# A turn's sum of squares in the second input projection: two additions on GpSimd, one product with ones, made in the next turn

## What is computed

```python
proj = h @ w_in                       # split into q_lat, kv_lat, k_rope, x_lru, g_lru
xc = conv1d(x_lru, conv_w) + conv_b   # four taps along the tokens
r = sigmoid(xc @ w_a + b_a); i = sigmoid(xc @ w_x + b_x)     # per head, blocks of 128
log_a = -8 * r * softplus(-lam);  a = exp(log_a)
b = sqrt(max(1 - exp(2 * log_a), 0)) * (i * xc)
hh = scan(a, b)                       # h[t] = a[t] * h[t-1] + b[t]
lru = hh * gelu(g_lru)                # 512 wide
mixed = concat(rms_norm(attn, attn_out_norm), rms_norm(lru, lru_out_norm))
```

## Time and profile before

| | us |
|---|---|
| median of 3 runs | 4268.16 |
| lowest, highest | 4266.77, 4273.60 |
| span of the profiled execution | 4260.5 |
| the stage `second_projection` in it | about 2348 to 2884 |

### The profile page before, as it was taken

The page is one execution under the profiler, slowest core; times in us unless marked ns, Lnnn a source line. Parts: engine busy times, 40 slices in busy tenths (PEclk is TensorE's granted clock), DMA queues, the critical chain, the costliest instruction groups (busy, mean ns, idle before and its releaser), DMA issues. The chain is left out here.

```text
span 4260.5 us, 53668 instructions
## 1 busy us (share of the span) xinstructions
PE 3916.6 (92%) x17927; PEld 2473.8 (58%) x17945; DVE 1735.5 (41%) x3722; ACT 1457.9 (34%) x3219; POOL 594.5 (14%) x757
## 2 busy tenths in 40 slices
PE   6999999799889977999998999969999897899998
PEld 4677667455765535777776777745666454333333
DVE  1343344566555550101111577773333445333332
ACT  1122122455444411111110566653333222344443
POOL 0000000100530011111111000000000001333332
PEclk8999999899999968999999999989999998899999
DMA  6221221222434566665654222132231233698963
GB/s 231 82 79 68 94 88 48 90 81 87 149 128 165 177 233 233 203 193 189 205 172 137 63 65 65 60 89 69 60 99 39 94 128 144 216 301 274 290 202 74
DMA packets 228403, 581.86 MB, mean 137 GB/s; under 512 B 28394, under 2 KB 99306, under 8 KB 212382
## 3 DMA queue, kind: packets, MB, share of 16 engines
q1 hardware_dynamic: 176702, 395.74, 27.1%
q0 software_dynamic: 51552, 184.18, 14.5%
HBM read 437.60 MB, written 142.12 MB: 136 GB/s over the span
## 5 line engine op out<-in xcount | busy, mean ns | idle before, releaser
L2135 PE MATMUL out_psO<-out_w,out_mixT 128*128 128x512 f32 x1024 | 449.6, 597 | 3.3 <-ACT out_mixT L2107 1.8
L878 PE MATMUL inp_psU<-inp_w,inp_hT 128*128 128x512 f32 (+3 forms) x1376 | 420.8, 464 | 0.0
L3968 PE MATMUL moe_psU<-moe_wu,moe_xT 128*64 x768 | 345.7, 604 | 6.4 <-issue 5.6
L3970 PE MATMUL moe_psU<-moe_bu,moe_xT 128*64 128x512 f32 x768 | 345.7, 604 | 0.0
L878 PEld LDWEIGHTS inp_psU<-inp_w,inp_hT 128*128 128x128 f32 x1376 | 256.0, 190 | 152.7 <-issue 122.4
L2135 PEld LDWEIGHTS out_psO<-out_w,out_mixT 128*128 128x128 f32 x1024 | 193.7, 192 | 237.1 <-issue 237.1
L874 PE MATMUL inp_psU<-inp_hT,inp_w 128*128 128x256 f32 x1088 | 242.1, 382 | 10.1 <-DVE inp_tm L680 4.5
L2609 PE MATMUL moe_psG<-moe_xT,moe_g_w 128*128 128x256 f32 x1024 | 234.5, 383 | 4.1 <-DMA moe_u_w<-in_w_up 4.1
L3329 PE MATMUL inp_psU<-inp_hT,inp_w 128*128 128x256 f32 x1024 | 230.2, 381 | 2.3 <-DMA inp_wg<-in_lru_wx 2.3
L2609 PE MATMUL moe_psG<-moe_xT,moe_u_w 128*128 128x256 f32 x1024 | 231.5, 379 | 0.0
L874 PEld LDWEIGHTS inp_psU<-inp_hT,inp_w 128*128 128x128 f32 x1088 | 206.5, 192 | 41.5 <-issue 3.9
(11 more groups left out here) (660 smaller groups left out, 6727.0 us busy)
## 6 DMA issues: line engine op xcount, KB each, us to landing
moe_wu<-in_w_up SPq DMA_DIRECT2D x32, 2048.0 KB, 17.9
moe_g_w<-in_w_gate SPq DMA_DIRECT2D x16, 2048.0 KB, 8.5
moe_u_w<-in_w_up SPq DMA_DIRECT2D x16, 2048.0 KB, 13.4
moe_d_w<-in_w_down SPq DMA_DIRECT2D x16, 2048.0 KB, 10.0
moe_wd<-in_w_down SPq DMA_DIRECT2D x32, 1024.0 KB, 19.8
mod_w<-in_w_ada SPq DMA_DIRECT2D x24, 1024.0 KB, 7.4
inp_mod_w<-in_w_mod SPq DMA_DIRECT2D x16, 1024.0 KB, 4.9
xn<-out_xn POOLq DMA_DIRECT2D x32, 512.0 KB, 3.8
```

The lines of the kernel that those rows point to most:

```text
L878: mm = pe.matmul(psU[:, u % NB, 0:n], hT[:, par, k, j * P:(j + 1) * P], w[:, k, lo:lo + n], start=(k == 0), stop=(k == KD - 1))
L2135: mm = pe.matmul(psO[:, j, h, :], mixT[:, j, k, :], out_weights.half[k // 4][:, k % 4, h * BANK:(h + 1) * BANK], start=(k == 0), stop=(k = ...
L3968: pe.matmul(psU[0:HALF, p, :], xT[:, p, k, 0:HALF], wu[:, bass.ds(slot, 1), k, :].rearrange("p a n -> p (a n)"), start=(k == 0), stop=(k = ...
L3970: mm = pe.matmul(psU[HALF:P, p, :], xT[:, p, k, HALF:P], bu[:, p, k, :], start=(k == 0), stop=(k == KD - 1), tile_position=(0, HALF))
```

## The change

GpSimd gets `square(b)`: it adds tiles 0 and 1 of the squares to tiles 2 and 3, and then the two sums, into a new buffer lo_sq. `sum_squares` makes a single product with ones from it, and is called behind unit 1 of the turn after the one in which it stood. `norm_root` on ACT and `finish` on DVE move accordingly: norm_root(g-2) behind keep_fm of the first pair, finish(g-2) behind mark(g-1). ACT's gate(b, 0), which writes r anew, waits for the first addition, and no longer for the squares. The order of the slots is as before.

```diff
+        lo_sq = s.sb("lo_sq", [P, LB // 2, G])
@@ vector, body
-                if late(g, 2):
-                    finish(g - 2)
                 if late(g):
                     norm_latents(g - 1)
                     convolve(g - 1, 1 - par)
                     mark(g - 1, 1 - par)
+                if late(g, 2):
+                    finish(g - 2)
                 if follows:
                     norm(g + 1)
@@ vector, behind the turns
-            finish(last - 1)
             norm_latents(last)
             convolve(last, last % 2)
             mark(last, last % 2)
+            finish(last - 1)
@@ scalar
             def gate(b, k):
                 if late(b) and k == 0:
-                    act.wait_ge(multiplied, b)
+                    act.wait_ge(sq_ch, b)
...
                 keep_fm(g, par, 0)
+                if late(g, 2):
+                    norm_root(g - 2)
...
                     keep_turned(b, 1)
-                    norm_root(b)
...
             root_latents(last)
+            norm_root(last - 1)
@@ tensor
             def sum_squares(b):
                 to = free(b, "N")
-                pe.wait_ge(multiplied, b + 1)
-                for k in range(LB):
-                    mm = pe.matmul(to[:, 0:G], K["ones"][:, :], r[:, k, :], start=(k == 0), stop=(k == LB - 1))
-                mm.then_inc(slotted, 1)
+                pe.wait_ge(sq_summed, b + 1)
+                pe.matmul(to[:, 0:G], K["ones"][:, :], lo_sq[:, 0, :], start=True, stop=True).then_inc(slotted, 1)
 
             def beside(b, u):
 
+                if u == 1 and late(b):
+                    sum_squares(b - 1)
...
                 if u == 9:
                     turn_heads(b, 1)
-                    sum_squares(b)
...
             for u in range(NF + TB):
                 beside(last, u)
+            sum_squares(last)
@@ gpsimd
+            def square(b):
+
+                pool.wait_ge(multiplied, b + 1)
+                if late(b):
+                    pool.wait_ge(slotted, b * NS)
+                pool.tensor_tensor(lo_sq[:, :, :], r[:, 0:2, :], r[:, 2:4, :], ALU.add).then_inc(sq_ch, 1)
+                pool.wait_ge(sq_ch, b + 1)
+                pool.tensor_tensor(lo_sq[:, 0, :], lo_sq[:, 0, :], lo_sq[:, 1, :], ALU.add).then_inc(sq_summed, 1)
...
                 if late(g):
                     for j in range(TB):
                         put_v(g - 1, j)
+                    square(g - 1)
                     for j in range(TB):
                         put_turned(g - 1, j)
```

More of the change, by code:

```diff
@@ L2770, in second_projection @@
                  "lifted", "rotated", "v_ready", "kept", "gch", "a_ready", "m2_ready", "m_in", "m_ready", "g_ready", "multiplied", "norm_rooted",
-                 "fch", "final", "passed", "pos_used")
+                 "fch", "final", "passed", "pos_used", "sq_ch", "sq_summed")
         (fixed, zeroed, dch, rooted, x_scaled, turned, hT_ready, unit, fm_kept, tm_kept,
@@ L2775, in second_projection @@
          lifted, rotated, v_ready, kept, gch, a_ready, m2_ready, m_in, m_ready, g_ready, multiplied, norm_rooted,
-         fch, final, passed, pos_used) = (s.sem(n) for n in names)
+         fch, final, passed, pos_used, sq_ch, sq_summed) = (s.sem(n) for n in names)
         x_landed = [s.sem(f"x_landed{j}") for j in range(TB)]
@@ L3383, in _ @@
                 put_v(last, j)
+            square(last)
             for j in range(TB):
```

## The result

The changed kernel takes 4288.99 us (median of five runs, 4284.37 to 4291.62) against 4268.73 of before: a ratio of 1.0041, with a 95% interval of 1.003 to 1.0052. I had forecast 4262 and no measurable change. It is slower, and lies beyond the range. The profiled execution has a span of 4288.7 us and took 4290.56.

The account below looks back on a forecast made before the run. The prediction took each turn as bound by a ring through PE, ACT and DVE. Its terms, -0.9 + 0.7 - 5.5 - 0.6 = -6.3 us, against the median 4268.16 gave 4262 us, range 4255 to 4275.

Parts of the forecast that it names:

- PE's pause before unit 0: Between turns, PE's wait ahead of the next turn's first unit grows from 1.46 to about 3.2 us.
- rival D: PE's clock halves behind the longer pause, deciding between 3.4 and 4.6 us; with held copies 4280.6, slower; chance 0.10.
- rival B: Between turns POOL's first addition holds DVE's edges copy, 0.9 to 1.05 us in seven passages, +6.7, 4268.5; chance 0.25.
- a turn's end: One product instead of four there lets unit 0 start earlier, at 2640.1 instead of 2641.04: -0.91 us.
- Convolve, squares of x and gates: Times into a turn: convolve starts at 7.5 us, squares of x at 19.0, gates 2 and 3 at 27.1.
- -1.3 for turn 3: In turn 3 the table load of norm_root no longer stands behind its wait on ACT: -1.3 us once.
- Turns of 60.9: Length in us forecast for a turn of the changed stage; turns 2 to 6 gain +0.4 each.
- POOL's additions: GpSimd's two additions of squares take 1.05 and 0.6 us, and POOL has the time for them.
- Drain, first part: After turn 7, norm_latents(7) no longer stands behind finish(6): -5.5 us, the largest term.
- last part: At the drain's end, two PE records instead of eight save 2.8 us, POOL's additions and handovers cost 2.1: -0.6.
- C: ACT takes later roots without delaying gates 2 and 3, saving 0.85 us in five turns: 4257.6; chance 0.15.
- E: The drain's gain of 5.5 us is lost, finish(6) or POOL's stores being late there: 4267.4; chance 0.08.

Follow-up runs that it names:

- drain_only: Kernel before with one move alone: behind turn 7, finish(6) stands behind mark(7) instead of ahead of norm_latents(7); 4265.81 us, ratio 0.9989.
- after_again: The changed kernel measured and profiled once more, nothing altered; 4289.94 us, ratio to before 1.0036.
- late_pool: The changed kernel, but GpSimd's additions also wait for DVE's two token-major copies, except behind turn 7; 4279.06 us, ratio to before 1.0017.
- relaxed: The changed kernel, but convolve no longer waits for the product with ones, only for the earlier slots of the turn before; 4278.38 us, ratio to before 1.0015.
- four_moved: The changed kernel without GpSimd's additions: four products with ones straight from the squares, at the new place behind unit 1; 4283.87 us, ratio to before 1.0026.
- edged_pool: The changed kernel, but GpSimd's additions also wait for DVE's edges copy, not for the token-major copies; 4281.13 us, ratio to before 1.0025.
- best0: The changed kernel with the edges copy ahead of the scan and convolve not waiting for the product with ones, no filler; 4272.04 us, ratio to before 0.9998.
- filled: The changed kernel with six unused products of ones filling PE's pause at the end of each turn from 1 on with a next one; 4272.58 us, ratio to before 0.9997.
- best2: best0 plus two unused products of ones as filler in PE's pause between turns; 4263.60 us, ratio to before 0.9980.
- best4: best0 plus four unused products of ones as filler in PE's pause between turns; 4263.84 us, ratio to before 0.9982.
- one_product: Kernel before with one product with ones, of tile 0 alone, instead of four at the old place; nothing moved, no GpSimd additions; 4268.65 us, ratio 0.9997.

## Why the prediction was wrong

**The step that failed: PE's longer pause was costed at nothing.** The pause itself I had right: "PE's pause before unit 0 grows from 1.46 to about 3.2 us" (3.18 and 3.26 measured; behind held passages 4.04 to 4.25, and 3.14 behind turn 1). What it does I took from one row, the 3.44 us pause of the earlier trace rows behind which PE ran at full clock, and put the point of decision "between 3.4 and 4.6". At that very place the changed kernel paused 2.57 us and ran at 0.50. The other kernels, which are the same program up to there, say the same: the clock fell behind eleven pauses of 2.03 to 4.94 us at this place, in drain_only behind 3.41, and stayed up behind two of 1.31 and 1.40. In this stage the clock fell behind 42 of 42 pauses of 2.10 to 4.27 us (six each in the change, after_again, late_pool, relaxed, four_moved, edged_pool and best0). The row was an exception, and the chance of 0.10 for rival D hung on it.

The trace of the kernel before could have told. Two of its other pauses, each with the stretch behind it:

```profile
1512.62 3.59 PE L2163 MATMUL out_psL<-out_wr,out_h2T 128*128 128x16 f32 x16 [2.56 <-ACT out_h2T L2116]
1512.62:1516.62 4.00, 4.00 (x19) 4.00 (x20) 0.92 (x2) 0.32 (x2) 1.06 (x2) 0.50 0.97 399
...
3104.94 1.16 PE L3537 MATMUL lata_psO<-lata_v,lata_pT 128*128 128x128 f32 x8 [2.36 <-DVE lata_o L3583]
3104.94:3108.94 4.00, 4.00 (x24) 2.93 (x24) 1.46 (x5) 2.04 (x5) 1.08 (x2) 1.00 0.19 33
```

It has seven pauses of 2.0 to 4.7 us that begin at full clock and have dense work of PE on both sides, through nearly all of 4 us. The clock fell behind four (2.02, 2.56, 2.56 and 4.62) and stayed up behind three (2.36, 2.36 and 3.44). So from before's own rows a fall behind 3.2 us was about as likely as not, and not a matter of 0.10, and the point of decision doesn't lie between 3.4 and 4.6.

Price by filled, from turn 1 on: 498.4 - 484.8 = **+13.5**; I had named 12 for six passages.

**The collision**, rival B: its price of 0.9 to 1.05 was right (1.04), and so was its reason; it came in five passages of seven, 5 x 1.04 = **+5.2**. I had given it 0.25, because DVE might "come first by a hair". In five of seven POOL came first, by 0.07 to 0.08.

**The rest of the sum** held, to 0.3 in a turn and 1.3 in the drain. -0.91 for a turn's end: -0.96 (late_pool, turn 1); the terms as shown, 2641.04 less 2640.1, give -0.94. Convolve, squares of x and gates at 7.5, 19.0 and 27.1: 7.65, 19.1, 27.06 in filled. -1.3 for turn 3: turn 3 of filled is as long as turn 5. Turns of 60.9: 60.6 to 60.7. POOL's additions, 1.05 and 0.6: 1.25 and 0.72, hidden as I said. Drain, first part -5.5: -5.5 in drain_only, -4.4 in the change; last part -0.6 (its terms, 2.8 less 2.1, give -0.7): from the end of the last squares to the attention 15.2 before and 14.7 now, -0.4.

**The sum again.** -6.3 forecast. With 1.3 less for the drain, 5.2 for the collision, 13.5 for the clock, and 0.8 off because turns 2 to 6 of filled are shorter than my terms make them, it is +12.9; measured from turn 1 on +12.7. (Some 0.4 of the drain's 1.3 are in the clock's price too.) Rivals B and D together, "-6.3 + 6.7 + 12", = +12.4, were the case that came, 0.3 short. The other 8 us between their 4280.6 and the median lie ahead of turn 1 or outside the stage, and no run places them.

**C** (the ring doesn't close over ACT) is out: gate 2 without a wait ahead of it, in the change as in filled. **E** is out by drain_only.

## What to carry to other kernels

Work of PE that fills a wait between two dense stretches isn't free to remove: in this stage its four products kept the clock up, and taking them away cost 1.7 us and more a turn where it saved 0.96. Before shortening such a stretch, compute the pause that it leaves, and look at every pause of that size in the trace, not at one; a filler without use, put where PE waits anyway, gave the loss back. And where two engines answer one signal, ask which inputs each reads from SBUF: moving the small SBUF copy out of that place, ahead of the scan, made the additions free of the critical path.

## What the runs showed of the hardware

- In this stage PE's granted clock fell to 0.50 behind all 42 pauses of 2.10 to 4.27 us between dense stretches: from 1.7 us before the restart to 1.4 us after it, and it was back 3.0 to 6.2 us after the restart. Like pauses led to short and long slow stretches. Elsewhere it isn't every time: of seven such pauses in the kernel before three left the clock up, the longest of 3.44 us.
- With a filler ahead of them, pauses of 1.2 to 1.5 us (best2), 0.4 to 0.6 (best4) and 0.6 to 1.7 (filled) let it fall in none of eighteen; without one, neither 1.31 nor 1.40 in the first stage (after_again, best2). With 1.43 of pause, 0.45 of work and 0.23 of pause (one_product) it fell once in six. In the second block's attention a pause of 1.76 us (L3537 of before) let it fall in before and drain_only and in none of the other twelve, so no pause of that order is safe by these rows.
- In this stage DVE's edges copy and POOL's addition excluded each other by order of start, with 0.07 to 0.08 us enough: POOL first, and the copy of 0.17 takes 1.21; both at once, and POOL's addition takes 1.30 instead of 1.25. DVE's copies from PSUM weren't touched. The 1.19 us of the earlier trace rows, with DVE first by 0.11, is the one row against that order.
- GpSimd adds 128x512 float32 in 1.25 us and 128x256 in 0.72 where no DVE instruction slows it; beside the latents' sums (late_pool) the first takes 1.41 to 1.44.
